# Two sets of TensorE transposes in a hybrid decoder step replaced by VectorE block transposes with GpSimd and ScalarE copies

## The reference: what is computed

```
xn = rms_norm(x);  proj = xn @ w_in                      # 1024 -> 8200 columns, three head groups
mLSTM (4 heads x 256):  h = (w_inter * q C + (q k^T * weights) v) / max(|den|, exp(-m))
                        h = sigmoid(o) * h;  rms_norm per head;  y_ml = h * silu(z)
                        C = decay * C + k^T v             # state carried from chunk to chunk
conv (512):             y_cv = b * conv3(c * xc) * silu(z_cv)
memory attention (4 heads x 128, 256 memory tokens):
                        p = softmax(qx mem_k^T / sqrt(128));  y_xa = (p mem_v) * silu(z_x)
y = x + [y_ml, y_cv, y_xa] @ w_out;   final rms_norm
```

## Time and profile before

| | |
|---|---|
| median of 3 runs | 2020.84 us (2015.42 to 2021.22) |
| profiled execution | 2021.7 us, span 2019.8 us |
| TensorE busy | 2008.2 us (99%), granted clock 9 tenths or more in all 40 slices |
| VectorE busy | 1474.5 us (73%) |
| ScalarE busy | 912.9 us (45%) |
| GpSimd busy | 874.6 us (43%) |
| chain that ended last | TensorE 93%, VectorE 2%, SP's queue 2%, DMA 1% |

### The profile page before, as it was taken

One profiled execution on the slowest core, in us unless ns is written; L12 is line 12 of the kernel. 1 busy time (PEld: TensorE's weight loads), 2 busy tenths in 40 slices (PEclk: granted clock), 3 DMA queues, 4 the chain that ended last, 5 costly groups with the idle time before them and its releaser, 6 DMA issues.

```text
span 2019.8 us, 34158 instructions
## 1 busy us (share of the span) xinstructions
PE 2008.2 (99%) x12151; PEld 1877.8 (93%) x12151; DVE 1474.5 (73%) x2336; ACT 912.9 (45%) x1863; POOL 874.6 (43%) x721
## 2 busy tenths in 40 slices
PE   9999999999999999999999999999999999999998
PEld 6999999999999999999999999998888888888886
DVE  7777787798778877897778767654445468777775
ACT  5554445445444455454454455442324333433332
POOL 2556555585555565575555555520000122222220
PEclk9999999999999999999999999999999999999999
DMA  6655667555646676555445566578746788888765
GB/s 205 155 142 142 150 152 162 128 141 124 152 122 152 158 171 134 137 143 122 120 131 138 126 157 144 134 212 188 172 115 183 201 250 261 272 239 237 235 180 121
DMA packets 600151, 333.69 MB, mean 165 GB/s; under 512 B 331296, under 2 KB 563888, under 8 KB 599984
## 3 DMA queue, kind: packets, MB, share of 16 engines
q1 hardware_dynamic: 561824, 312.90, 59.5%
q10 hardware_dynamic: 37008, 14.43, 2.9%
q0 software_dynamic: 1152, 4.19, 0.6%
HBM read 237.87 MB, written 93.58 MB: 164 GB/s over the span
## 4 chain that ended last, share of the span: by engine, by line
PE 93%; DVE 2%; SPq 2%; DMA 1%; issue 1%; ACT 0%; POOL 0%; DVEq 0%; POOLq 0%; ACTq 0%
PE bank L742 21%; PE bank L744 21%; PE bank L743 21%; PE bank L2294 3%; PE bank L2296 2%; PE bank L2295 2%; PE bank L2264 2%; PE bank L2249 2%; PE bank L1650 1%; PE bank L1651 1%; PE bank L1652 1%; PE bank L1636 1%; PE bank L1639 1%; PE bank L1637 1%; PE bank L1601 1%; PE bank L1566 1%
## 5 line engine op out<-in xcount | busy, mean ns | idle before, releaser
L742 PE MATMUL bank<-xh,wh 128*128 128x352 f32 x2688 | 869.3, 323 | 0.9 <-DVE stage L1111 0.9
L744 PE MATMUL bank<-xh,wl 128*128 128x352 f32 x2688 | 867.0, 323 | 0.0
L743 PE MATMUL bank<-xl,wh 128*128 128x352 f32 x2688 | 863.6, 321 | 0.0
L1093 DVE TENSOR_TENSOR wl<-raw,wh 128x512 fp32r<-128x512 f32 x384 | 407.4, 1063 | 166.5 <-ACT wh L881 165.5
L742 PEld LDWEIGHTS bank<-xh,wh 128*128 128x128 f32 x2688 | 504.6, 188 | 3.8 <-issue 2.0
L743 PEld LDWEIGHTS bank<-xl,wh 128*128 128x128 f32 x2688 | 507.4, 189 | 0.3 <-issue 0.2
L744 PEld LDWEIGHTS bank<-xh,wl 128*128 128x128 f32 x2688 | 506.3, 188 | 0.0
L903 ACT ACTIVATE snap<-bank 128x352 f32<-128x352 f32 x384 | 178.5, 465 | 374.3 <-PE bank L744 374.2
L881 ACT ACTIVATE wh<-raw 128x512 fp32r<-128x512 f32 x384 | 240.6, 628 | 156.8 <-PE bank L744 155.6
L1093 DVE TENSOR_TENSOR wl<-wt,wh 128x512 fp32r<-128x512 f32 x288 | 246.8, 860 | 85.1 <-ACT wh L881 84.2
L692 POOL TENSOR_TENSOR stage<-snap 128x352 f32<-128x352 f32 x96 | 100.8, 1050 | 440.7 <-ACT snap L903 428.1
(11 more groups left out here) (346 smaller groups left out, 2599.0 us busy)
## 6 DMA issues: line engine op xcount, KB each, us to landing
raw<-in_w_in SPq DMA_DIRECT2D x72, 1024.0 KB, 5.8
raw<-in_w_in SPq DMA_DIRECT2D x48, 512.0 KB, 5.6
scr_vob<-stage SPq DMA_DIRECT2D x192, 88.0 KB, 3.6
scr_qk<-stage SPq DMA_DIRECT2D x48, 352.0 KB, 5.2
raw<-scr_qk SPq DMA_DIRECT2D x16, 1024.0 KB, 8.8
area<-scr_vob SPq DMA_DIRECT2D x32, 512.0 KB, 8.0
scr_acc<-x_res SPq DMA_DIRECT2D x17, 512.0 KB, 6.2
m_acc<-scr_acc SPq DMA_DIRECT2D x17, 512.0 KB, 7.6
```

The lines of the kernel that those rows point to most:

```text
L742: pe.matmul(out, wh[:, b, k, :], xh[:, b, k, :], start=(first and k == 0), stop=False, skip_group_check=True)
L743: pe.matmul(out, wh[:, b, k, :], xl[:, b, k, :], start=False, stop=False, skip_group_check=True)
L744: m = pe.matmul(out, wl[:, b, k, :], xh[:, b, k, :], start=False, stop=(k == 3), skip_group_check=True)
L1093: dve.tensor_tensor(low, source(q, b), high.bitcast(F32), ALU.subtract).then_inc(S["w_low"], 1)
```

## The change

**In attend**, 12 of the 18 jobs (all but the first two, the two sample jobs and the job behind each) are no longer transposed by TensorE. VectorE transposes the whole of `pr` in 32x32 blocks into a spare 1024-column slot of `raw` (`turn_blocks`, one instruction of 128x1024, placed behind `xa_low(t)`); then 16 copies of 32 partitions by 256 elements carry each row and column of blocks to its place in `pT`: 10 on GpSimd, 6 on ScalarE (`p_moves`, ahead of `conv_high`). `weigh_values` waits for all 16. The slot is taken from the ring of key buffers, which has three slots instead of four. The load of the second q and k tile moves from iteration 14 to 15 and waits for all block copies.

**In recur**, 14 of the 16 tiles (1 to 14) are turned in the same way: VectorE turns `th` into `kb` (`turn_y`, one 128x1024 instruction), 8 copies of 32x256 on ScalarE (behind `keys(t+1)`, ahead of `unit_front`) and 8 on GpSimd carry the blocks back into `th`, and `y_gate` reads SBUF instead of PSUM. To make h earlier, VectorE's order changes in these tiles: behind j = 5 now stand `turn_keys(t+1)` and `second_half(t)`, behind j = 6 `turn_y`, behind j = 7 `final_norm(t-2)`. The load of `kb` for tile t+2 waits for the copies of tile t.

More of the change, by code:

```diff
@@ L1454, in attend, with turned_by_pe, turned_in_blocks @@
     s_at = [at["s", 0], at["s", 1]]
+    by_pe = [n for n, (kind, t) in enumerate(jobs) if n < 2 or "s" in (kind, jobs[n - 1][0])]
+    by_block = [n for n in range(len(jobs)) if n not in by_pe]
+    POOL_MOVES = [(g, f) for g in range(4) for f in range(4)][:10]
+    ACT_MOVES = [(g, f) for g in range(4) for f in range(4)][10:]
+    def turned_by_pe(n):
+        return sum(x < n for x in by_pe)
+    def turned_in_blocks(n):
+        return sum(x < n for x in by_block)
+    def p_block(tile, part, column):
+        return tile[SQ * part:SQ * (part + 1), :, :, SQ * column:SQ * (column + 1)]
     def due(t):
@@ L1548, in _, with load_values @@
         pool.wait_ge(S["mask_ready"], 3)
-        for b in range(DB):
+        def load_values(b):
+            if b >= DB:
+                return
             if b == 0:
@@ L1582, in turn_p @@
         def turn_p(n):
+            if n in by_block:
+                return
             pe.wait_ge(S["p_ready"], 4 * n + 4)
-            wait(pe, S["pT_ready"], 2 * n)
+            wait(pe, S["pT_ready"], 2 * turned_by_pe(n))
             for g in range(4):
@@ L1711, in exps @@
             act.wait_ge(S["nb_ready"], n + 1)
-            wait(act, S["p_turned"], 2 * n)
+            wait(act, S["p_turned"], 2 * turned_by_pe(n))
+            wait(act, S["p_squared"], turned_in_blocks(n))
             for g in range(4):
@@ L1804, in turn_keys @@
                 return
-            dve.wait_ge(S[f"s_K_loaded{b % 4}"], 64 * (b // 4 + 1))
-            dve.transpose(KT[:, b, :, :].rearrange("p h s -> p (h s)"), ksq[:, b % 4, :]).then_inc(S["s_KT_ready"], 1)
+            dve.wait_ge(S[f"s_K_loaded{b % 3}"], 64 * (b // 3 + 1))
+            dve.transpose(KT[:, b, :, :].rearrange("p h s -> p (h s)"), ksq[:, b % 3, :]).then_inc(S["s_KT_ready"], 1)
         def xa_low(t):
@@ L1891, in _ @@
         pool.wait_ge(S["acc_stored0"], 16)
-        for b in range(4):
-            pool.wait_ge(S[f"s_K_loaded{b}"], 64 * 2)
+        for b in range(3):
+            pool.wait_ge(S[f"s_K_loaded{b}"], 64 * (3 - b // 2))
         for a in range(2):
@@ L1959, in unit, with turned_by_pe @@
         return u // 4, u % 4
+    def y_moved(t, a, f):
+        return th[t % 2].rearrange("p (k x) -> p k x", k=KM)[SQ * f:SQ * (f + 1), :, SQ * a:SQ * (a + 1)]
+    def turned_by_pe(t):
+        return 2 * sum(x not in IN_BLOCKS for x in range(t))
     def split_y(t):
@@ L2189, in _ @@
         for t in range(NT):
+            if t - 1 in IN_BLOCKS:
+                pool.wait_ge(S["y_carried"], len(POOL_MOVES) * (t - 1))
             ahead(t + 1)
@@ L2208, in turn_keys @@
                 pe.wait_ge(before["exp_ready"], 4 * (NT + 2))
-                pe.wait_ge(before["pT_ready"], 2 * (NT + 2))
+                pe.wait_ge(before["pT_ready"], 2 * 6)
             wait(pe, S["t1_ready"], 4 * t)
@@ L2242, in numerators @@
                         pe.wait_ge(S["kw_ready"], 4 * t + 2 * h + 2)
-                else:
-                    wait(pe, S["y_gated"], 2 * (t - 1) + h - 1)
+                elif t == 1:
+                    pe.wait_ge(S["y_gated"], h - 1)
+                elif h == 2:
+                    wait(pe, S["s_vo_ready"], sum(front_of(x) is not None for x in range(t)))
                 num = bank[1 + h][:, 0:HE]
@@ L2690, in turn_o @@
             wait(dve, S["s_squared"], units_before(t))
-            wait(dve, S["y_turned"], 2 * (t - 1))
+            wait(dve, S["y_gated"], 2 * (t - 1))
             dve.transpose(th[t % 2], vo[:, 1, :]).then_inc(S["o_turned"], 1)
```

22 lines of the change are left out of this document (13 added, 9 removed).

## The result

The changed kernel takes 2039.76 us (median of 6 runs, 2037.14 to 2044.67). The kernel before, run beside it, takes 2021.03 (2015.42 to 2024.06). The ratio is 1.0094, 95% interval 1.0082 to 1.0107: slower by 18.7 us, where 2017.6 was forecast and 2031 was the upper end of the range. The profiled execution took 2037.14, with a span of 2035.3.

A forecast was written before the change was run, and what follows sets the result against it. TensorE, 99% busy, was taken as the bound, unless chains through other engines close a tile later. Attend -5.2, between stages +0.5, recur +1.5: -3.2 from the profiled 2021.7 gives 2018.5, less 0.9 to the median, 2017.6 us; range 2006 to 2031.

The forecast's parts named there:

- The ceiling and the prices: Removed transposes: 0.87 us per attend job, 0.91 per recur tile, at most 23.2 us; plus prices of added transposes and copies.
- attend: the loop: Six key-load tiles, 1 to 5 and 7: ScalarE's issues, copies and convolution make a 15.5 to 15.9 us loop, priced 0.
- The far end, +0.6: Worst case for each of attend's six key-load tiles: 0.6 us slower; best case 0.87 us faster.
- The other six tiles: Attend's block tiles without key loads: full gain of 0.87 us each, 5.2 us together, bounds 3 to 5.2.
- what lies between the stages: Second q and k load moves behind SP's last residual load: cost 0 to 3 us, 0.5 taken.
- recur, numerators: Numerators still wait for score_weights: gain 0.09 us of 0.87 at odd tiles' ends, at most 0.49 of 0.91 at even.
- recur, even tiles: Slower y_gate and late score_weights use up VectorE's slack before update 1; per tile bounds 0.5 us gain, 2.6 loss.
- The term of -0.2 per even tile: The gain of 0.2 us taken for each of seven even recur tiles.
- recur, odd tiles: VectorE's new order makes update 6 late, so TensorE's update 8 comes 0.5 us late in 7 tiles: +3.5 us.
- Rival 2: GpSimd's copies at 0.70 to 0.83 us delay recur's even tiles, TensorE waits at update 1: 2035 us, chance 0.22.
- the chances: Whole kernel: faster (below 2014.8 us) 0.36, slower (above 2026.9) 0.22, the rest 0.42.

The follow-up runs named there:

- e7_even: The whole change with outputs turned in blocks only in the even recur tiles 2 to 14, odd tiles by TensorE as before: 2034.83 us, ratio 1.0063 to the kernel before.
- e5_scores_early: e3_hold with TensorE's scores of the next tile moved one product group ahead: 2022.59 us, ratio 0.9998 to the kernel before.
- e3_hold: The whole change plus one wait: GpSimd starts work ahead for tile t+2 only after VectorE's y_low of tile t: 2026.03 us, ratio 1.0022 to the kernel before.
- e6_best: e5_scores_early with all block copies on GpSimd in attend's key-load tiles and update 8 one product group later: 2006.85 us, ratio 0.9914 to the kernel before.

## Why the prediction was wrong

**The ceiling and the prices: right, but for GpSimd's copies.** Where TensorE doesn't wait, an attend interval falls by the 0.87 that was counted (15.30 to 14.42, 9.88 to 9.01). ScalarE's copies: six in 2.61 and eight in 3.49 us, forecast 2.5 and 3.3. The block transpose: 1.24. GpSimd's copy, forecast 0.38 between 0.29 and 0.83: ten in 4.45 us, some 0.45 each (6.7 us for the ten in tiles 11 to 14, where VectorE splits weights beside them, and hidden there too). In recur eight took 4.47 instead of 3.04: some 0.5 of that is the price, and 0.9 is one copy that was held to 1.31 us beside final_norm. The prediction had final_norm held instead; it took its usual 1.27. y_gate was late by 0.63, forecast 0.2.

**attend: the loop right, its size short, one tile missed.** Key-load tiles were put at 15.5 to 15.9 and priced at nothing; they took 15.8 to 16.3, 0.5 to 0.8 over the same tiles before, since the issues held ScalarE longer, 5.26 us and not 4.75 in the tile shown. The far end, +0.6, was nearer. Tile 7 I took for one of these six. Its loop is the same, from a gate at 1464.31 to one at 1479.73, but behind a tile with two jobs TensorE has less of its own to do in it:

```profile
1479.37 0.47 PE L1675 MATMUL bank<-convw,out_yh 128*128 128x512 f32 x1 [3.01 <-DVE x_res L1909]
```

That interval is 19.3 us instead of 15.3. Of these 4.0 us, 1.6 are a fallen clock (below): in e7_even, with the same attend and the same wait, 3.03 us, but without the fall, it is 17.7. The other six tiles gave what was forecast only in part: intervals of 15.3 became 14.4 and 9.9 became 9.0, but that of tile 11 went from 15.3 to 15.8. There the six copies stand behind wm_high until 1539.29, conv_low starts at 1539.98 instead of 1537.36, and TensorE waits 1.12 us for the residual add; as in tile 7, it has less work of its own behind a tile with two jobs. Sum +2.4 with what lies between the stages, instead of -4.7.

**recur, numerators: right in mechanism.** They wait 0.68 us behind an odd tile and 0.31 behind an even one, for score_weights. From the start of the scores to the numerators: 2.87 us before and 2.84 after behind an odd tile, a gain of 0.03 where 0.09 was put; 3.27 and 2.84 behind an even one, a gain of 0.43 where 0.49 was possible and 0.2 taken. e5_scores_early shows the cause by removing the wait.

**recur, even tiles: the step that failed.** "y_gate now reads two SBUF inputs too, beside GpSimd's mask sum: 1.28 becomes some 1.8", VectorE up to 0.6 late, slack used up, bounds down to a loss of 2.6, and a gain of 0.2 taken. Measured: 2.90. I had taken the 0.54 us by which y_low's pair was slower as the price of a contested pair. GpSimd's timeline beside that row, in the kernel before:

```profile
1770.76 1.28 POOL L2143 TENSOR_TENSOR work<-area,mask 128x512 f32<-128x512 f32 x1 [10.85 <-DVE work L2618]
1772.67 1.07 POOL L2147 TENSOR_TENSOR m_wide<-raw,area 128x256 f32<-128x256 f32 x1 [0.64 <-PE bank L2250]
1773.97 0.91 POOL L2147 TENSOR_TENSOR m_wide<-raw,area 128x256 f32<-128x256 f32 x1 [0.23 <-PE bank L2250]
```

The mask sum lay beside y_gate there too, and y_gate, from PSUM, took its usual 1.28. Of y_low's two instructions the first took 0.69 and only the second, 1.22, was held: 0.54 was the price of one instruction. And GpSimd stood idle before each product, for TensorE's numerators. In the kernel after, the mask sum comes behind GpSimd's copies, 0.9 us later than the numerators instead of 0.4 ahead of them, and the products follow it without a gap. So all four instructions of VectorE are held, the first of them 1.1 us beside the mask sum (1.76) and the three others 0.53 each beside a product (1.21), and y_low, which I left at 1.83, grew as well.

The term of -0.2 per even tile was +1.5 in five tiles: from the numerators to the next scores an odd tile takes 25.77 us after and 23.80 in e3_hold, 1.97 less, and the 0.43 of the numerators goes against it. In tile 2 y_gate ran alone and the wait was 0.85; in tile 14 GpSimd has no work ahead left, all four instructions ran alone, and there was no wait. e3_hold took the waits away and gave back 13.7 us.

The Trainium skill, SBUF — State Buffer, "Who interferes with whom", was quoted in the prediction as a stricter reading, and read for y_gate alone. Its rule, that a VectorE instruction with two SBUF inputs contends with a GpSimd instruction that reads SBUF, is borne out by the traces, on both sides: VectorE's instructions take 0.68 to 0.69 us alone and 1.2 to 1.8 contested, GpSimd's products 0.73 alone and 1.18 contested. The weight that I gave it against one row was too small.

**recur, odd tiles: right in place, nearly in size.** Update 8 was put 0.5 us late; it waits 0.39 in the traced tile and 3.2 us over seven. Each stop costs more than the idle time in brackets, though (below): from update 7 to unit_update it is 1.56 us before and 2.22 in e3_hold, so this stop costs 0.66, and with the restarts at the numerators and update 1 the odd tile is 0.85 longer even with the gates undisturbed (22.95 against 23.80). Seven times 0.85, the even tiles' 5 x 1.54 and 3.3 for two intervals with a fallen clock make up the 17 us of this stage; the rest cancels.

**Rival 2 was right in place and in number, wrong in its mechanism, and the number was luck.** It named TensorE waiting at update 1 and 2035, worked out from copies of 0.70 to 0.83 us; they took 0.45, and with the held one 0.56 on average, for which its own figures (0.8 us a tile at 0.5, some 2.4 at 0.70) give about 2027, an estimate. e3_hold leaves the copies alone and the wait vanishes. Had I stopped at the trace after, this rival would have looked confirmed. The copies have a part all the same: they make y_gate up to 0.63 us late, and by the timelines they move GpSimd's work ahead to where it is in VectorE's way. No run takes only the copies from GpSimd, so the second of these is read, not shown.

**What came on top.** Two odd intervals have a fallen clock, 1.6 and 1.7 us (below), and one of attend. And the chances were laid out badly: the working itself said that the slack of 0.6 us was used up and that an even tile could lose 2.6, seven times, against a gain of at most 0.5; slower should have had more than 0.22.

## What to carry to other kernels

When an edit moves an operand of VectorE from PSUM to SBUF, list what GpSimd runs in the same microseconds and count every VectorE instruction with two SBUF inputs in that stretch, not only the edited one, as one that can be held by a GpSimd instruction (or hold it, as final_norm did a copy); then look how much slack its successor has. Work taken from the bounding engine is a gain only if something else covers the wait that it covered: move other independent work into its place in the same edit. A list that is nearly as long as the tile on an engine at 28% to 37% busy, such as ScalarE's in attend with its DMA issues, is a bound in waiting, and two short moves (copies elsewhere, or issues elsewhere) each lift it.

## What the runs showed of the hardware

**A stop of TensorE costs more than its bracket shows.** TensorE around an even tile's end in the kernel before, then in e3_hold:

```profile
1769.85 0.53 PE L2362 MATMUL bank<-m_wide,m_s_kp 128*128 128x32 f32 x4
1770.21 1.07 PE L2342 MATMUL bank<-ident,area 128*128 128x128 f32 x8
```

```profile
1769.83 0.53 PE L2443 MATMUL bank<-m_wide,m_s_kp 128*128 128x32 f32 x4
1770.67 0.67 PE L2330 MATMUL bank<-m_wide 128*128 128x257 f32 x2 [0.31 <-issue]
```

From the four small matmuls to whatever follows is 0.36 us in a full queue and 0.84 with the stop: 0.48 lost, 0.31 of it shown. The other 0.17 is the overlap of consecutive matmuls, which the busy time contains. With 14 stops at the numerators alone this is over 2 us.

**The granted clock fell behind some of the long waits.** Windows of 10 us of the kernel after (columns as above; the clock is the third number from the end):

```profile
1470.00:1480.00 10.00, 6.99 (x40) 5.96 (x39) 4.75 (x12) 4.93 (x15) 1.82 (x5) 1.00 0.56 136
1480.00:1490.00 10.00, 10.00 (x39) 8.14 (x38) 5.45 (x8) 4.16 (x10) 3.92 (x10) 0.83 0.49 160
1730.00:1740.00 10.00, 8.13 (x29) 6.54 (x29) 6.79 (x22) 4.59 (x13) 2.68 (x6) 0.83 0.79 177
```

The lower of the two levels is 1.2 GHz; from 1480.67 on matmuls of 512 columns started 0.43 us apart instead of 0.23, for part of the window. What it costs stands in the intervals: the two long odd ones are 1.6 and 1.7 us above the others. TensorE had stood idle for 3.01 us before the first (1479.37) and 1.87 before the second (1732.04). Three of the five waits of 1.9 us had no such fall behind them, nor had the 3.03 us of e7_even, so what decides is left open. In e3_hold, e5_scores_early and e6_best, without these waits, recur has no fallen interval.
